# A hybrid attention, mLSTM and PEER step: 384 instead of 448 dense columns, the whole last prompt tile by fetched expert rows, and other shapes for three transfers

## The reference

```python
xn = rmsnorm(xp, norm1_g[l])
(aq, ak, av), (mq, mk, mv, ig, lf), mo, ga, gb = _project(xn, w_in[l], b_in[l], ml_f_bias[l])
att = chunk_attention_prompt(aq, ak, av, att_rel_bias[l])
(Cn, nn_, mn), h = mlstm_prompt(mq, mk, mv, ig, lf)
xp = xp + _merge(att, h, mo, ga, gb, w_att_branch[l], w_ml_branch[l], w_out[l])
xp = xp + peer_ffn(rmsnorm(xp, norm2_g[l]), peer_wq[l], peer_sub_keys[l], peer_u[l], peer_v[l])
```

```python
s = jnp.einsum('nhpd,hpkd->nhpk', q, sub_keys)
sv, si = lax.top_k(s, PEER_TOPK)
cand = sv[:, :, 0, :, None] + sv[:, :, 1, None, :]      # 16 x 16 sums, flattened
fv, fi = lax.top_k(cand, PEER_TOPK)
g = jax.nn.softmax(fv, axis=-1)
u, vv = expert_u[eidx], expert_v[eidx]                  # eidx from si and fi
act = jax.nn.gelu(jnp.einsum('nhkd,nd->nhk', u, xb), approximate=False)
return jnp.einsum('nhk,nhkd->nd', g * act, vv)
```

## Time and profile before

| | us |
|---|---|
| median of 3 runs | 2185.53 (2179.06 to 2189.41) |
| profiled execution, its own time | 2187.16 |
| its span | 2185.4 |
| PE busy | 2011.7 (92%) |
| DVE busy | 1282.9 (59%) |
| ACT busy | 918.6 (42%) |
| POOL busy | 797.6 (36%) |
| moved by DMA | 421.7 MB, 193 GB/s over the span |

### The profile page before, as it was taken

How to read it: one execution, slowest core, us unless ns; L and a number is a source line. 1 busy time by engine, 2 the same in 40 slices (tenths; PEclk the granted TensorE clock), 3 DMA queues, 4 the chain that set the end, 5 groups by cost and what they waited for, 6 DMA issues and landing times. The chain is left out here.

```text
span 2185.4 us, 32122 instructions
## 1 busy us (share of the span) xinstructions
PE 2011.7 (92%) x11629; PEld 1826.0 (84%) x11629; DVE 1282.9 (59%) x2482; ACT 918.6 (42%) x2008; POOL 797.6 (36%) x780
## 2 busy tenths in 40 slices
PE   7299987998996999999999999996999999999997
PEld 6298876886895998898999999996989889998896
DVE  2014352334613299999999855552566666666666
ACT  4012112224314233585888888882333323323333
POOL 4142322322321201485898888880011111111110
PEclk9699988999997999999999999998999999999999
DMA  6431135222606166788889899988679879889873
GB/s 150 71 87 39 39 127 91 81 77 89 210 20 137 41 178 184 203 256 239 254 233 264 247 265 265 259 255 271 221 253 293 284 252 298 284 273 298 269 252 108
DMA packets 304465, 421.70 MB, mean 193 GB/s; under 512 B 32116, under 2 KB 248692, under 8 KB 300724
## 3 DMA queue, kind: packets, MB, share of 16 engines
q1 hardware_dynamic: 276660, 318.98, 50.4%
q0 software_dynamic: 27648, 100.68, 15.0%
HBM read 346.43 MB, written 72.42 MB: 192 GB/s over the span
## 5 line engine op out<-in xcount | busy, mean ns | idle before, releaser
L1311 PE MATMUL ps<-x_high,uT_high 128*128 128x448 f32 x1024 | 383.9, 375 | 15.8 <-DVE uT_low L1303 15.8
L1888 PE MATMUL ps<-hid_high,v_high 128*128 128x448 f32 x1024 | 376.9, 368 | 22.8 <-DVE hid_low L1861 22.8
L1555 POOL TENSOR_SCALAR area<-iota_row,chosen 128x128 f32<-128x128 f32 x448 | 376.5, 854 | 2.6
L1888 PE MATMUL ps<-hid_low,v_high 128*128 128x448 f32 x1024 | 375.7, 367 | 0.0
L1888 PE MATMUL ps<-hid_high,v_low 128*128 128x448 f32 x1024 | 375.7, 367 | 0.0
L1311 PE MATMUL ps<-x_high,uT_low 128*128 128x448 f32 x1024 | 375.3, 367 | 0.0
L1311 PE MATMUL ps<-x_low,uT_high 128*128 128x448 f32 x1024 | 374.9, 366 | 0.0
L1834 ACT CAST v_high<-area 128x1024 fp32r<-128x1024 f32 x128 | 134.2, 1048 | 448.2 <-PE ps L1888 369.7
L1229 POOL DMA_INDIRECT gathered_rows<-in_peer_v_dram,gathered_index x96 | 96.8, 1009 | 570.1 <-DVE gathered_acc L1261 481.5
L1859 DVE TENSOR_TENSOR v_low<-area,v_high 128x1024 fp32r<-128x1024 f32 x128 | 156.8, 1225 | 233.7 <-ACT v_high L1834 233.7
L1303 DVE TENSOR_TENSOR uT_low<-u_turned,uT_high 128x1024 fp32r<-128x1024 f32 x128 | 159.3, 1244 | 158.8 <-ACT uT_high L1298 158.8
(11 more groups left out here) (289 smaller groups left out, 3731.5 us busy)
## 6 DMA issues: line engine op xcount, KB each, us to landing
u_nat<-in_peer_u_dram SPq DMA_DIRECT2D x512, 128.0 KB, 4.7
area<-in_peer_v_dram SPq DMA_DIRECT2D x128, 512.0 KB, 5.3
hidden<-gelu_out SPq DMA_DIRECT2D x128, 224.0 KB, 3.3
routing<-dense SPq DMA_DIRECT2D x28, 1024.0 KB, 6.1
w_raw<-in_w_in_dram SPq DMA_DIRECT2D x44, 512.0 KB, 4.0
area<-hidden SPq DMA_DIRECT2D x8, 1792.0 KB, 8.6
gelu_in<-hidden SPq DMA_DIRECT2D x8, 1792.0 KB, 9.5
routing_in<-routing SPq DMA_DIRECT2D x8, 1792.0 KB, 16.7
```

What stands on the lines that cost most here:

```text
L1311: ins = self.nc.tensor.matmul(self.k.ps[:, b, 0:N], w[:, b, kk, :], x[:, kk, 0:N], start=(kk == 0 and p == 0), stop=(kk == KD - 1 and p == 2))
L1555: ins = nc.gpsimd.tensor_scalar(first[:, b % AREAS, f, :], iota[:, :], chosen[:, 0, c:c + 1], None, ALU.is_equal)
L1888: ins = nc.tensor.matmul(ps[:, kk, 0:N], v[:, b, kk * P:(kk + 1) * P], h[:, b, :], start=(n == 0 and p == 0), stop=(n == P - 1 and p == 2))
```

## The change

Five things are changed.

- **Store of rel_line**: in 8 pieces (`PIECES`), one after each weight load from tile 5 to tile 12, each 16 of the 128 copies. The waits ask for all 8.
- **u and wq loads**: a u load takes 32 rows and spreads their four quarters over 128 partitions (256 values each), instead of one quarter of 128 rows on 32 partitions; still 4 transfers of 128 KB. peer_wq is loaded in 16 transfers over 128 partitions instead of 8 over 32.
- **Whole last prompt tile fetched**: `MORE` becomes a list of pieces of tile 3, here one of all 128 frames; `HALVED` is 0, N = 384. Its picks are 128 row columns, so `ALL` = 32 + 128 = 160. The batches of routing fall from 112 to 96, the transfers of hidden and routing shrink from 448 to 384 columns. Tile 3's routing is not computed.
- **Row additions**: spread over steps 7 to 120 of the experts stage, so that `added` follows (n - 6) * ALL / 114.
- `posf` and `picked` move into the unused end of `area1`, to make room.

The number of copies for which is waited (`COPIES`) follows. In the rows of the order below line numbers of the two kernels differ; what is at L1239, L1261, L1291 and L1303 before stands at L1246, L1268, L1298 and L1310 now.

A step without an add is now one with an add, and two of five have two; the tensors beside are a seventh narrower. The core of the diff:

```diff
-FETCHED = P // 2
-SETS = P // FETCHED
-HALVED = P - FETCHED
+MORE = [(0, P)]
+HALVED = min(lo for lo, _ in MORE)
 N = 3 * P + HALVED
...
+PIECES = 8
 AHEAD_LOADS = 64 if HALVED else 48
-MORE = PH * TOPK // SETS
-ALL = PICKS + MORE
+SETS = [P // f for _, f in MORE]
+TAKEN = [PH * TOPK // n for n in SETS]
+FROM = [PICKS + sum(TAKEN[:j]) for j in range(len(MORE) + 1)]
+ALL = FROM[-1]
+COPIES = 2 * sum(SETS)
...
                 load_tile(i)
-                if i == 5:
-
-
+                if 5 <= i < 5 + PIECES:
                     sp.wait_ge(line_done, 1)
-                    sp.dma_start(k.line_dram, bcast(line, 1, P)).then_inc(line_stored, 16)
+                    rows = slice((i - 5) * P // PIECES, (i - 4) * P // PIECES)
+                    sp.dma_start(k.line_dram[:, rows], bcast(line, 1, P // PIECES)).then_inc(line_stored, 16)
...
-            sp.wait_ge(line_stored, 16)
+            sp.wait_ge(line_stored, 16 * PIECES)
...
-            dve.wait_ge(line_stored, 16)
+            dve.wait_ge(line_stored, 16 * PIECES)
...
-        for a in range(QUARTERS):
-            sp.dma_start(self.u_nat[a * BLK:(a + 1) * BLK, v, :].rearrange("i (g d) -> i g d", g=P // BLK),
-                         self.peer_u[0, n * P:(n + 1) * P, a * D // QUARTERS:(a + 1) * D // QUARTERS].rearrange("(g i) d -> i g d", i=BLK)
+        for g in range(QUARTERS):
+            rows = n * P + g * BLK
+            sp.dma_start(self.u_nat[:, v, g * 256:(g + 1) * 256], self.peer_u[0, rows:rows + BLK, :].rearrange("i (a d) -> a i d", a=QUARTERS)
                          ).then_inc(self.u_loaded[v], 16)
...
-                for a in range(QUARTERS):
-                    sp.dma_start(w[c][a * BLK:(a + 1) * BLK, :, :],
-                                 peer_wq[0, a * D // QUARTERS:(a + 1) * D // QUARTERS, c * 512:(c + 1) * 512].rearrange("(b j) n -> j b n", j=BLK)
+                for b in range(KD):
+                    sp.dma_start(w[c][:, b, :], peer_wq[0].rearrange("(a b j) n -> a b j n", a=QUARTERS, j=BLK)[:, b, :, c * 512:(c + 1) * 512]
                                  ).then_inc(wq_loaded[c], 16)
...
-                if n >= 8 and n % 5 != 0 and (n - 8) * 4 // 5 < ALL:
+                while added[0] < min(ALL, (n - 6) * ALL / (P - 14)):
                     gathered.add(dve, added[0])
                     added[0] += 1
...
-                    for c in range(2):
-                        ins = nc.tensor.matmul(ps[HALVED:P, 2 * t + c, :], same[:, TS:], gathered.acc[:, 1, c * 512:(c + 1) * 512], start=True, stop=True)
+                    for j, (lo, frames) in enumerate(MORE):
+                        cols = slice(TS + lo - HALVED, TS + lo - HALVED + frames)
+                        for c in range(2):
+                            ins = nc.tensor.matmul(ps[lo:lo + frames, 2 * t + c, :], same[:, cols], gathered.acc[:, 1 + j, c * 512:(c + 1) * 512],
+                                                   start=True, stop=True)
```

More of the change, by code:

```diff
@@ L109, in program @@
         k.ones = keep("ones", [P, P])
-        k.same = keep("same_frame", [P, TS + FETCHED])
+        k.same = keep("same_frame", [P, TS + P - HALVED])
         k.x = keep("x", [P, NT, D])
@@ L157, in program @@
             hold = holder(last)
-            gathered.acc = hold("gathered_acc", [P, 2, D])
+            gathered.acc = hold("gathered_acc", [P, 1 + len(MORE), D])
             k.acc = hold("acc", [P, KD, N])
@@ L1231, in fetch, with part @@
                                           ).then_inc(self.fetched[m % RING], 16)
+    @staticmethod
+    def part(m):
+        return sum(m >= f for f in FROM[:-1])
     def arrived(self, eng, m):
@@ L1238, in dot @@
         row = self.rows[:, m % RING, :]
-        self.nc.vector.scalar_tensor_tensor(out=row, in0=row, scalar=1.0, in1=self.x[:, 0 if m < PICKS else 1, :], op0=ALU.mult, op1=ALU.mult,
+        self.nc.vector.scalar_tensor_tensor(out=row, in0=row, scalar=1.0, in1=self.x[:, self.part(m), :], op0=ALU.mult, op1=ALU.mult,
                                             accum_out=self.pre[:, m:m + 1]).then_inc(self.used, 1)
@@ L1367, in _ @@
                 sp.dma_start(gathered.x[g * TS:(g + 1) * TS, 0, :], gathered.x[0:TS, 0, :]).then_inc(gathered.x_ready, 16)
-            sp.wait_ge(row_scaled, 2)
-            for g in range(SETS - 1):
-                sp.dma_start(gathered.x[g * FETCHED:(g + 1) * FETCHED, 1, :], gathered.x[HALVED:P, 1, :]).then_inc(gathered.x_ready, 16)
-            sp.wait_ge(gathered.x_ready, 16 * (EXTRA - 1 + SETS - 1))
+            sp.wait_ge(row_scaled, 1 + len(MORE))
+            copies = EXTRA - 1
+            for j, (lo, frames) in enumerate(MORE):
+                for g in range(SETS[j]):
+                    if g * frames != lo:
+                        copies += 1
+                        sp.dma_start(gathered.x[g * frames:(g + 1) * frames, 1 + j, :], gathered.x[lo:lo + frames, 1 + j, :]).then_inc(gathered.x_ready, 16)
+            sp.wait_ge(gathered.x_ready, 16 * copies)
         @block.scalar
@@ L1442, in _ @@
                                            op0=ALU.mult, op1=ALU.mult).then_inc(row_scaled, 1)
-            nc.vector.scalar_tensor_tensor(out=gathered.x[HALVED:P, 1, :], in0=x[HALVED:P, 3, :], scalar=k.rstd[HALVED:P, 3:4], in1=g2_row[HALVED:P, :],
-                                           op0=ALU.mult, op1=ALU.mult).then_inc(row_scaled, 1)
+            for j, (lo, frames) in enumerate(MORE):
+                rows = slice(lo, lo + frames)
+                nc.vector.scalar_tensor_tensor(out=gathered.x[rows, 1 + j, :], in0=x[rows, 3, :], scalar=k.rstd[rows, 3:4], in1=g2_row[rows, :],
+                                               op0=ALU.mult, op1=ALU.mult).then_inc(row_scaled, 1)
             nc.vector.tensor_reduce(k.same[:, 0:TS], ident[:, :].rearrange("p (g t) -> p t g", g=EXTRA), AX.X, ALU.add)
-            nc.vector.tensor_reduce(k.same[:, TS:], ident[:, :].rearrange("p (g t) -> p t g", g=SETS), AX.X, ALU.add)
+            for j, (lo, frames) in enumerate(MORE):
+                cols = slice(TS + lo - HALVED, TS + lo - HALVED + frames)
+                nc.vector.tensor_reduce(k.same[:, cols], ident[:, :].rearrange("p (g t) -> p t g", g=SETS[j]), AX.X, ALU.add)
             for n in range(2):
@@ L1515, in step @@
                     sp.wait_ge(pick_done, 1)
-                    for g in range(SETS):
-                        half, picks = slice(g * FETCHED, (g + 1) * FETCHED), slice(g * MORE, (g + 1) * MORE)
-                        sp.dma_start(gathered.index[half, PICKS:], flat[HALVED:P, picks]).then_inc(gathered.more_ready, 16)
-                        sp.dma_start(gathered.weight[half, PICKS:], picked[HALVED:P, 2, picks]).then_inc(gathered.more_ready, 16)
+                    for j, (lo, frames) in enumerate(MORE):
+                        rows, mine = slice(lo, lo + frames), slice(FROM[j], FROM[j + 1])
+                        for g in range(SETS[j]):
+                            to, picks = slice(g * frames, (g + 1) * frames), slice(g * TAKEN[j], (g + 1) * TAKEN[j])
+                            sp.dma_start(gathered.index[to, mine], flat[rows, picks]).then_inc(gathered.more_ready, 16)
+                            sp.dma_start(gathered.weight[to, mine], picked[rows, 2, picks]).then_inc(gathered.more_ready, 16)
                 for b in plan.routing.get(n - 3, []):
```

22 lines of the change are left out of this document (12 added, 10 removed).

## The result

The changed kernel takes **2501.08 us** (median of 4 runs, 2497.88 to 2507.0), against 2184.11 us for the kernel before on the same chip: a ratio of 1.1454, 95% interval 1.1417 to 1.1491. The forecast was 2119 us. The wrong sign needs one explanation, and the gains that were forecast need a second one, since they don't show even when the first cause is taken out.

A forecast was written before the change was run, and what follows sets the result against it. PE was taken to set the pace in search steps 80 to 120 and experts, DVE as full in steps 16 to 80, with PE idle in the front. Terms summed to -67 us, giving 2119 us from 2187.2 - 67 - 1.6; range 2095 to 2145.

The forecast's parts named there:

- search, 0 to 16: First 16 search steps: DVE busy 73 of 83 us with hardly any dots; forecast -2 us.
- to the experts: Search steps 120 to 128 and passage to experts: waits on transfers and last routing, each a seventh smaller; -6 us.
- Start of the PEER part: wq and u loads over all partitions: 672 to 695 us: loads over all partitions run faster, so ACT's wait for wq nearly goes; -6 us (0 to -8).
- Front, -32: Front, 64 to 105 us: store in pieces lets weight loads through, PE idling falls from 41 to 10 us; -32 us.
- Rival C: Front: pieces don't free the weights, PE idles as long in all, front term 0; 2151 us, chance 0.09.
- Search, 16 to 80, +38: Search steps 16 to 80: 38 more dots on DVE, column saving hidden; 424 us against 386, +38 us.
- Search, 80 to 120, -15: Search steps 80 to 120: fewer columns shorten PE's work, DMA then takes 222 us; -15 us (-27 to +8).
- Experts, -42: Experts stage: eight steps fall from 40.2 to 38 us at 348 GB/s; -42 us (-89 to +20).
- Rival A: Experts stage: DMA isn't the bound, groups of eight go by PE at 34.6 us; 2072 us, chance 0.13.
- D (the ring): Experts stage: ring of three fetched rows becomes the bound, kernel slower; 2208 us, chance 0.08.
- B (the clock): Search: PE idling behind DVE lowers its clock, +33 us; 2152 us, chance 0.12.

The follow-up runs named there:

- light POOL: Changed kernel with old u and wq loads, POOL building one of four one-hots per batch from the fifth batch on: 2147.04 us.
- spread order: Large experts-stage loads in six parts, one behind each v load: changed kernel with old u and wq loads 2165.63 us; kernel before with store in pieces 2117.06 us.
- fourth buffer: Changed kernel with old u and wq loads and a ring of 4 fetched rows instead of 3: 2227.57 us.
- thin dots: Changed kernel with old u and wq loads, 2 of every 5 dot products on DVE reading 64 of 1024 columns: 2158.52 us.
- plain loads over 128 partitions: Changed kernel with u loads of one expert row per partition, source beginning with a dimension of 128, wq loads in new form: 2207.87 us.
- Fetches into 64 partitions: Changed kernel with old u and wq loads, each experts-stage fetch bringing rows of 64 partitions instead of 128: 2192.93 us.

## Why the prediction was wrong

Each term against what it came to in the traces, in us; "mended" is the changed kernel with the old loads.

| term | forecast | changed | mended |
|---|---|---|---|
| front and wq | -32 - 6 | -38.5 | -53.7 |
| search, 0 to 16 | -2 | +20.2 | -5.4 |
| 16 to 80 | +38 | +177.0 | +39.1 |
| 80 to 120 | -15 | +128.1 | +31.3 |
| to the experts | -6 | +16.5 | +0.7 |
| experts and end | -42 - 2 | +7.1 | +4.6 |
| sum | -67 | +310.4 | +16.6 |

**The step that failed** is "Start of the PEER part: wq and u loads over all partitions". It took the rate of loads that span all partitions from the earlier trace rows, gave the new loads "a rate between the two", and asked only how many partitions the SBUF side has. It never asked how many engines a transfer with 4 entries in its first dimension gets. It had the number in hand: it had read the 0.47 of the rel_line store as half the engines because "its source is still 8 partitions", and did not carry this to the pattern two edits further. And it had priced the u loads' new shape at nothing in the search stage, where 4 of them stand in every step. For the term it gave bounds of 0 and -8, and none of its four rivals lets these loads be slower. 310.4 - 16.6 = 294 of the 310 us are this step: the new loads ran at 100 GB/s on 4 engines, the wait for wq grew from 6.89 to 17.78 us, and a step of the search from 6.0 to 8.8 us. The rest of the miss, from -67 to +16.6 us, is in the two stages further down.

**Front, -32**: right in mechanism, too small; the pieces alone gave -46. PE is busy 40.26 of the 41 us that it idled before. That front and wq together came to -38.5, as forecast, is luck: the pieces brought more and the wq loads cost what they were to bring. (The kernels with pieces and old wq loads have fronts of 693.1 to 702.5 us, so the -53.7 of the mended one holds some scatter.) Weight tiles came faster than the 10 us apart that I had worked out: hardly later than the 7.6 us of a piece alone, so the loads ran beside the pieces. (That PE needs a tile every 5.8 us was also slightly off: the product written there is 5.9.) POOL, three tiles in a row, 7.9 us apart:

```profile
71.08 1.04 POOL L472 CAST w_high<-w_raw 128x1024 fp32r<-128x1024 f32 x1 [3.88 <-DMA w_raw<-in_w_in_dram]
...
78.97 1.04 POOL L472 CAST w_high<-w_raw 128x1024 fp32r<-128x1024 f32 x1 [4.38 <-DMA w_raw<-in_w_in_dram]
...
86.87 1.04 POOL L472 CAST w_high<-w_raw 128x1024 fp32r<-128x1024 f32 x1 [4.39 <-DMA w_raw<-in_w_in_dram]
```

No wait for w_raw over 10 us, as the prediction asked. Rival C (the pieces don't free the weights) is out.

**Search, 16 to 80, +38**: right in its reason, DVE as the bound and the columns' saving hidden, once the old loads are back. That it is right to 1 us is luck: DVE is busy 407 us and not 412, and idles 18 us and not 12. And the light POOL shows that POOL has a part of 20 us in the stage, which the term didn't have.

**Search, 80 to 120, -15**: wrong with the old loads too, at +31. The step weighed PE, DVE and DMA and left out POOL, which had been busy 208.05 of 237 us in the earlier trace rows and got 22 fetches more, at the 1.12 us that a fetch had there before 25 us, against 16 fewer batches, which all lie elsewhere: 198 and 199 one-hots stand in this stretch. 208 + 25 = 233 us, more than the 222 that were forecast, and it was 248 in the end. That POOL was nearly full was in the rows. The upper bound of the term was also added up wrong: the 72 MB that it worked with take 254 us at the 285 GB/s that it named, +17 and not +8.

**Experts, -42**: the price came true, 38 us a group at 348 GB/s forecast, 38.3 at 346 measured, but only with the spread order, and there it isn't shown that the traffic is the bound. The middle 112 steps came to +19 us as the kernel was changed, and +17 mended. What failed is the sentence that put the group at 38 us from shares of DMA time: it took the traffic as if it could be moved in any order. A v load waits in the same queue behind 3 MB, and at 0.93 share nothing makes up for it. Rival A (PE as the bound, 34.6 us a group) is out: PE is busy 0.86 of the stage with the old order and 0.91 with the spread. D (the ring) is out with the old order by the fourth buffer, and open with the spread. B (the clock) is in part there, 0.93 with the old loads and 0.85 in the changed kernel in steps 16 to 80. I take it for a consequence, as PE idles 77 of the 425 us; with thin dots it is 0.95 and the stage is 34 us shorter. No run holds the clock apart.

What is left open, beside the bound of the experts after the spread: how short steps 80 to 120 get with lighter dots and a lighter POOL together, and a form of the whole tile with lighter POOL work that computes all of the result. It wasn't built. If it made the search as short as the light POOL did, which leaves three of four one-hots out, then by the stages (405 + 229 + 536) it would come near 2105 us, an estimate.

## What to carry to other kernels

Count the engines of a transfer before its bandwidth: look at the first dimension of both sides, and read the queue's share of 16 engines where it runs alone. 26% was four engines here, though the tile has 128 partitions. A low DMA share with long waits for data is the sign to look for.

A load that is needed soon must not stand behind a burst in the same queue: the same bytes in parts between the small loads gave 44 us here, and 17 in the kernel before, at a DMA share of 0.86. And where work is moved onto a stage, add it up for every engine in the stage's row, the quiet one too.

## What the runs showed of the hardware

Loads whose source began with a dimension of 4 ran at 100 GB/s and a share of 26.2%, and kept the same 4 engines busy. The loads over 32 partitions moved 287 GB/s for a full share beside other traffic, plain loads over 128 partitions 340 in the same mix: 18% more, not twice. Fetches into 64 partitions moved 254 against 352 GB/s, and the loads beside them, unchanged, 285 against 337. A mean of 346 GB/s at a share of 0.98 held for 536 us. POOL's one-hots of 128x128 had spans of 792 to 1152 ns on the mean in steps 80 to 120 of four kernels; a busy time of POOL is no fixed cost times a count.
